# Activations rounded once where a norm makes them, token projections in rounded parts, and experts taken four at a time

## The reference

```python
# first_block, per layer
h = rmsnorm(x, norm1_g[l]);  p = h @ w_in[l]
y_rw, y_ret, y_sg = rwkv7_branch(p_rw, ...), retention_branch(p_ret, ...), sgu_branch(p_sg, ...)
x = x + jnp.sum(sigmoid(gate_logits) * proj(y_rw, y_ret, y_sg), axis=2) @ w_out[l]
x = x + conv_ffn(rmsnorm(x, norm2_g[l]), ffn_w_up[l], ...)
# second_block
u = rms_norm(x, mix_norm_g) @ w_in          # conformer convolution and dilated attention
x = x + mixed @ w_out
x = x + memory_cross_attention(rms_norm(x, xattn_norm_g), rms_norm(mem, mem_norm_g), w_q, w_k, w_v, w_o)
x = x + hierarchical_moe(rms_norm(x, moe_norm_g), ...)
```

## Time and profile before

| | before |
|---|---|
| median of 3 runs | 4093.9 us (4088.15 to 4098.93) |
| the profiled execution's own time | 4100.52 us |
| its span, first to last instruction | 4098.5 us |
| busy: TensorE, its weight loads | 81%, 58% |
| busy: DVE, ACT, POOL | 33%, 23%, 23% |
| mean granted TensorE clock, share of 2.4 GHz | 0.893 |
| read from HBM | 398.42 MB, mean 98 GB/s |

### The profile page before, as it was taken

The page is one execution under the profiler, slowest core; times in us unless marked ns, Lnnn a source line. Parts: engine busy times, 40 slices in busy tenths (PEclk is TensorE's granted clock), DMA queues, the critical chain, the costliest instruction groups (busy, mean ns, idle before and its releaser), DMA issues. The chain is left out here.

```text
span 4098.5 us, 51376 instructions
## 1 busy us (share of the span) xinstructions
PE 3321.2 (81%) x20124; PEld 2357.0 (58%) x20125; DVE 1336.1 (33%) x2111; ACT 936.4 (23%) x1279; POOL 949.0 (23%) x640
## 2 busy tenths in 40 slices
PE   6497668979998759665997999739786777999997
PEld 5296455657876638534665887427334655554553
DVE  2643332124420274333113441261752232122122
ACT  2322211124421232121112442211232121000001
POOL 2020002324442311100322444111201322212220
PEclk9698779999999879877998999869788887999999
DMA  2001111212231100111222223011002203888884
GB/s 96 11 4 53 47 64 62 87 67 83 95 113 50 59 5 24 41 47 54 92 72 67 98 93 112 21 43 63 0 0 72 103 31 136 344 353 339 330 330 168
DMA packets 53861, 402.60 MB, mean 98 GB/s; under 512 B 7249, under 2 KB 8273, under 8 KB 14417
## 3 DMA queue, kind: packets, MB, share of 16 engines
q1 hardware_dynamic: 53712, 400.54, 25.6%
HBM read 398.42 MB, written 2.10 MB: 98 GB/s over the span
## 5 line engine op out<-in xcount | busy, mean ns | idle before, releaser
L232 POOL TENSOR_TENSOR w_lo<-w,w_hi 128x1024 fp32r<-128x1024 f32 (+1 forms) x268 | 725.0, 2709 | 2024.1 <-ACT w_hi L227 2024.1
L250 PE MATMUL bank<-rhs_hi,w_hi 128*128 128x512 f32 (+1 forms) x2016 | 542.3, 414 | 227.1 <-DVE rhs_hi L238 191.1
L250 PEld LDWEIGHTS bank<-rhs_hi,w_hi 128*128 128x128 f32 x2016 | 393.1, 198 | 340.3 <-issue 215.5
L227 ACT CAST w_hi<-w 128x1024 fp32r<-128x1024 f32 (+1 forms) x268 | 302.8, 1137 | 1028.4 <-PE bank L259 910.8
L255 PE MATMUL bank<-rhs_lo,w_hi 128*128 128x512 f32 (+1 forms) x2016 | 509.1, 396 | 31.0 <-DVE rhs_lo L241 31.0
L259 PE MATMUL bank<-rhs_hi,w_lo 128*128 128x512 f32 (+1 forms) x2016 | 496.8, 389 | 0.0
L255 PEld LDWEIGHTS bank<-rhs_lo,w_hi 128*128 128x128 f32 x2016 | 383.6, 193 | 120.9 <-DVE rhs_lo L241 42.8
L259 PEld LDWEIGHTS bank<-rhs_hi,w_lo 128*128 128x128 f32 x2016 | 380.1, 191 | 78.3
L1988 PE MATMUL bank<-moe_w,moe_hg 128*64 128x512 f32 x1024 | 222.9, 592 | 0.8 <-issue 0.8
L2081 DVE TENSOR_TENSOR xT<-xT,bank 128x512 f32<-128x512 f32 x128 | 87.8, 686 | 238.5 <-PE bank L2033 238.2
L1988 PEld LDWEIGHTS bank<-moe_w,moe_hg 128*64 128x64 f32 x1024 | 88.3, 137 | 131.8 <-issue 131.8
(11 more groups left out here) (372 smaller groups left out, 4054.4 us busy)
## 6 DMA issues: line engine op xcount, KB each, us to landing
moe_w<-in_moe_w SPq DMA_DIRECT2D x128, 1024.0 KB, 12.6
moe_w<-in_moe_w SPq DMA_DIRECT2D x32, 2048.0 KB, 12.5
w<-in_w_in SPq DMA_DIRECT2D x45, 1024.0 KB, 4.9
w<-in_ffn_up SPq DMA_DIRECT2D x44, 1024.0 KB, 4.9
w<-in_w_merge SPq DMA_DIRECT2D x24, 1536.0 KB, 6.5
w<-in_ffn_down SPq DMA_DIRECT2D x16, 1408.0 KB, 5.9
w<-in_w_out SPq DMA_DIRECT2D x24, 512.0 KB, 3.5
w<-in_w_xk SPq DMA_DIRECT2D x4, 1024.0 KB, 6.0
```

The source lines that it names most:

```text
L227: self.nc.scalar.copy(self.w_hi[:, t, :, :], raw).then_inc(self.sems["w_hi"], 1)
L232: self.nc.gpsimd.tensor_tensor(self.w_lo[:, t, :, :], raw, self.w_hi[:, t, :, :].bitcast(F32), ALU.subtract).then_inc(self.sems["w_lo"], 1)
L250: self.nc.tensor.matmul(bank, hi[:, t, k, :], self.rhs_hi[:, k, :], start=(k == 0), stop=False)
```

## The change

Three things are changed together.

1. **Parts from the norm.** `norm_phase` gets `parts=(hi, lo)`: DVE scales into a scratch tile, ACT casts the high part, DVE subtracts, tile by tile. The parts stay resident (`h_hi` over `hT`'s place, `h_lo` in a tile of its own) and go to all the phases that read this norm's result; these no longer call `split.rhs`. The output projections (`down_phase` with `merged`, `mixed`, `ox`) still split their own operand. The memory's norm writes parts 256 wide.
2. **Projection by tokens in parts.** The chunk is cut along the contraction: half t holds four of the eight feature tiles with all 256 columns. ACT casts and POOL subtracts a half; TensorE runs three products over it for all token tiles.
3. **Experts in fours.** `h_tok` becomes `h_hi` and `h_lo` (the latter over `T.w`, free by then). One gather serves four experts (256 selection columns, two rounded products for each pair of tiles). `selg` goes: the turned 0/1 selection scatters, y is multiplied by the slot's gate when it leaves PSUM and split in two parts, and the gates by slot come from one-column matmuls (`sum_gates`). The weights are still fetched pair by pair, by the same waits. Scatter is spread over the next up.

`rwkv_prep_phase` also puts its small weights `up` into slot 0 of `T.w` instead of a tile of its own. In the diff, `merge_phase` and `ffn_up_phase` change as `project_phase` does, and `step(k)` calls `scatter(g, k - 1)` for k = 1 to 6.

```diff
@@ norm_phase @@
             rsqrt(act, sems["rooted"], 0, rstd[:, :], T.ps[0][:, 0:width], 1.0 / (tiles * P), T.eps(eps))
+            if parts is not None:
+                for k in range(tiles):
+                    act.wait_ge(sems["scaled"], k + 1)
+                    nc.scalar.copy(parts[0][:, k, 0:width], sq[:, k, :]).then_inc(sems["hi_ready"], 1)
...
             for k in range(tiles):
-                nc.vector.scalar_tensor_tensor(out=dst[:, k, :], in0=src[:, k, :], scalar=gain[:, k:k + 1],
-                                               in1=rstd[:, :], op0=ALU.mult, op1=ALU.mult)
+                out = dst[:, k, :] if parts is None else sq[:, k, :]
+                nc.vector.scalar_tensor_tensor(out=out, in0=src[:, k, :], scalar=gain[:, k:k + 1],
+                                               in1=rstd[:, :], op0=ALU.mult, op1=ALU.mult).then_inc(
+                                                   sems["scaled"], 1)
+                if parts is not None and k > 0:
+                    dve.wait_ge(sems["hi_ready"], k)
+                    nc.vector.tensor_tensor(parts[1][:, k - 1, 0:width], sq[:, k - 1, :],
+                                            parts[0][:, k - 1, 0:width].bitcast(F32), ALU.subtract)
...
@@ project_phase @@
-        split = Split(nc, ctx, T, sems, kt, width=width)
+        split = Split(nc, ctx, T, sems, kt, *parts, width=width)
...
-            pe.wait_ge(sems["rhs_hi"], kt)
...
-            split.rhs(dve, rhs)
...
@@ token_project_phase @@
-                sync.wait_ge(sems["dve_took"], 2 * i + s + 1)
+                sync.wait_ge(sems["w_lo"], 4 * i + 2 * s + 2)
...
-                pe.wait_ge(sems["w_full"][s], 16 * i + 16)
                 pe.wait_ge(sems["act_took"], 2 * i + s + 1)
                 pe.wait_ge(sems["dve_took"], 2 * i + s + 1)
-                for m in range(tiles):
-                    for k in range(KD):
-                        mm = nc.tensor.matmul(T.ps[4 * s + m][:, 0:256], lhs[:, k, m * P:m * P + P],
-                                              T.w[:, s, k * 256:k * 256 + 256], start=(k == 0), stop=(k == KD - 1))
+                for t in range(2):
+                    n = 4 * i + 2 * s + t
+                    pe.wait_ge(sems["w_hi"], n + 1)
+                    for lhs, w in ((split.rhs_hi, w_hi), (split.rhs_lo, w_hi), (split.rhs_hi, w_lo)):
+                        if w is w_lo:
+                            pe.wait_ge(sems["w_lo"], n + 5)
+                        for m in range(tiles):
+                            for k in range(half):
...
+                                mm = nc.tensor.matmul(T.ps[4 * s + m][:, 0:256],
+                                                      lhs[:, half * t + k, m * P:m * P + P], w[:, t, k, :],
+                                                      start=first, stop=last)
...
@@ route_phase @@
             for m in range(4):
-                act.wait_ge(sems["turned"], 2 * m + 1)
-                nc.scalar.copy(M.h_tok[:, m, 0:512], T.ps[2 * (m % 2)][:, :]).then_inc(sems["act_took"], 1)
+                for half in range(2):
+                    act.wait_ge(sems["turned"], 2 * m + half + 1)
+                    nc.scalar.copy(M.h_hi[:, m, 512 * half:512 * half + 512],
+                                   T.ps[2 * (m % 2) + half][:, :]).then_inc(sems["act_took"], 1)
...
-                v.tensor_copy(M.h_tok[:, m, 512:1024], T.ps[2 * (m % 2) + 1][:, :]).then_inc(sems["dve_took"], 1)
+                    v.tensor_tensor(M.h_lo[:, m, o], T.ps[2 * (m % 2) + half][:, :], M.h_hi[:, m, o].bitcast(F32),
+                                    ALU.subtract).then_inc(sems["dve_took"], 1)
...
@@ experts_phase, TensorE @@
+            def gather(q, s):
+                pe.wait_ge(sems["sel_ready"], q + 1)
+                for n in range(4):
+                    pe.wait_ge((sems["hg_act"], sems["hg_dve"])[n % 2], 2 * q + n // 2 + 1)
+                    for k in (2 * n, 2 * n + 1):
+                        for m in range(4):
+                            for part in (M.h_hi, M.h_lo):
+                                mm = nc.tensor.matmul(hg_banks[n % 2][:, (k % 2) * W4:(k % 2) * W4 + W4],
+                                                      part[:, m, k * P:k * P + P], sel[:, s, m, :],
                                                      start=(m == 0 and part is M.h_hi),
                                                      stop=(m == 3 and part is M.h_lo))
+                    mm.then_inc(sems["gathered"], 1)
...
+            def scatter(g, k):
+                pe.wait_ge(sems["added"], KD * g + k + 1)
+                nc.tensor.matmul(add_banks[k % 2][:, :], y_hi[:, k * P:k * P + P], selT[:, :], start=True, stop=False)
+                nc.tensor.matmul(add_banks[k % 2][:, :], y_lo[:, k * P:k * P + P], selT[:, :], start=False,
+                                 stop=True).then_inc(sems["scattered"], 1)
...
+            for q, s, more in quads_and_more(pe):
+                for b in range(2):
+                    g = 2 * q + b
+                    if b == 1 and more:
+                        gather(q + 1, 1 - s)
+                        sum_gates(q + 1, 1 - s)
+                    turn_and_down(g, s, b)
...
+                        up(g + 1, 1 - b, step)
...
+                    scatter(g, 6)
+                    scatter(g, 7)
```

More of the change, by code:

```diff
@@ L359, in _, with token_project_phase, raw @@
                 write(nc.vector, 2 * i + s, 1, T.ps[2 * s + 1][:, 0:width]).then_inc(sems["dve_took"], 1)
-def token_project_phase(nc, T, sems, stale, weights, chunks, lhs, write, tiles=4, ahead=None):
-    with nc.Block() as block:
+def token_project_phase(nc, T, sems, stale, weights, chunks, parts, write, tiles=4, ahead=None):
+    half = KD // 2
+    with ExitStack() as ctx:
+        split = Split(nc, ctx, T, sems, KD, *parts)
+        w_hi, w_lo = (w.rearrange("p t k c -> p t (k c)").rearrange("p t (k c) -> p t k c", k=half)
+                      for w in (split.w_hi, split.w_lo))
+        block = ctx.enter_context(nc.Block())
+        def raw(s, t):
+            return T.w[:, s, t * half * 256:(t + 1) * half * 256].rearrange("p (k c) -> p k c", k=half)
         @block.sync
@@ L394, in _, with high @@
             act.sem_inc(sems["act_took"], 2)
-            for i, s in two_slots(act, chunks):
+            def high(i, s, t, first=False):
+                act.wait_ge(sems["w_full"][s], 16 * i + 16)
+                if not first and t == 0:
+                    act.wait_ge(sems["half_done"], 2 * i + s)
+                if not first and t == 1:
+                    act.wait_ge(sems["odd_done"], (2 * i + s) * (tiles // 2))
+                nc.scalar.copy(w_hi[:, t, :, :], raw(s, t)).then_inc(sems["w_hi"], 1)
+            high(0, 0, 0, first=True)
+            high(0, 0, 1, first=True)
+            for (i, s), behind in with_next(act, chunks):
+                if behind:
+                    high(*behind, 0)
                 for m in range(0, tiles, 2):
@@ L1102, with ffn_up_phase @@
 FFN_UP_SEMS = SPLIT_SEMS + " loaded gate_done val_done gate_taken val_taken conv_done silu_done made dve"
-def ffn_up_phase(nc, T, sems, stale, weights, layer, hT, made_hi, made_lo, ahead):
+def ffn_up_phase(nc, T, sems, stale, weights, layer, parts, made_hi, made_lo, ahead):
     done = (sems["gate_done"], sems["val_done"])
@@ new lines, in _ @@
+            gated(0)
+            for q, s, more in quads_and_more(dve):
+                for b in range(2):
+                    g = 2 * q + b
+                    if b == 1 and more:
+                        rows(q + 1, 1)
+                        rows(q + 1, 3)
+                    for half in range(2):
+                        o = slice(512 * half, 512 * half + 512)
+                        dve.wait_ge(sems["y_hi"], 2 * g + half + 1)
+                        nc.vector.scalar_tensor_tensor(out=y_lo[:, o], in0=y_banks[half][:, :],
+                                                       scalar=slot_gate[:, s, b:b + 1], in1=y_hi[:, o].bitcast(F32),
+                                                       op0=ALU.mult, op1=ALU.subtract).then_inc(sems["y_lo"], 1)
+                    for k in range(6):
+                        add(g, k)
+                    if b == 0 or more:
@@ L2118, in block_two @@
         part = lambda name, first=0: (lambda c: pick(d[name], c + first))
-        norm_phase(nc, T, norm2, norm, xT, gain("mix_norm_g_2"), hT, ahead=fetch_first(T, pa, chunk, part("w_in_2")))
+        norm_phase(nc, T, norm2, norm, xT, gain("mix_norm_g_2"), None, ahead=fetch_first(T, pa, chunk, part("w_in_2")),
+                   parts=parts)
         with nc.sbuf_tensor([P, KD, S], F32) as mixed:
```

369 lines of the change are left out of this document (205 added, 164 removed).

## The result

The kernel with the change takes 3938.7 us (median of 4 runs, 3935.0 to 3942.6); the kernel before, run beside it, 4093.1 (4 runs). The ratio is 0.9622 with a 95% interval of 0.9605 to 0.9639: 154 us or 3.8% faster. The forecast was 3905, with a range of 3872 to 3955. The profiled execution took 3935.0 us, its span 3933.2.

The account below looks back on a forecast made before the run. TensorE's work and its idle stretches between phases were taken as the bound, TensorE itself in the experts. Starts and norms 82, token projections 21 and experts 86 make 189: 4100.5 to 3911.5, as a median 3905; range 3872 to 3955.

Parts of the forecast that it names:

- Starts without a norm ahead: At phase starts, DVE's casts and subtractions go: 9.5, 7.2 or 11.5 us gained each, 2 at one, 82.3 in sum.
- the clock mostly stays: At gate and cross-attention query starts, the shortened gap mostly keeps TensorE's clock: 9.5 us gained each, some 8 if it falls.
- Rival 2: At phase starts, the clock falls in shortened gaps and ScalarE or SP is late: 82 becomes 40, 3947 us; chance 0.12.
- Norms: Norms that write parts take 11.3 us on the DVE, 5.9 longer; with what follows, -0.7 us together.
- Ahead of the FFN it is a draw: At the norm before the FFN, TensorE begins 5.9 us later but no longer stops 5.13 for a low part.
- Token projections: 416 f32 products each become three rounded ones at 0.120 us: 31 gained, net 21, bounds -34 and 27.
- rival 3: In token projections and gathers, weight loads aren't hidden at 256 columns: 197 us lost, 4102; chance 0.02.
- a warm tile takes 5.44 us: At phase starts, a tile at full clock was priced at 5.44 us, read from the trace before the change.
- Experts: In the experts, a quad takes 62.6 us, 31.3 a pair for 37.23: 86 gained, bounds 62 and 98.
- six of eight go between the steps of the next up: In the experts, scatter's 16 rounded products at 0.227 us take 3.6 for 7.87, most of them placed within up.
- the walk: In the experts, a quad's steps added up: 62.6 us, with 2.85 between up and down for its first pair, 12.7 second.
- Rivals 1, 4 and 5: Experts bound by transfers, 3945 us, chance 0.13; clock falls in experts, 4150, 0.03; weights or selections too late, 4090, 0.02.

Follow-up runs that it names:

- experiment 4: The change's kernel padded so that rounded weights and both resident parts begin at the same place modulo 256 bytes: 3921.5 us, ratio 0.9573.
- experiment 1: The change's kernel with the kernel before's route and experts: 4005.9 us, ratio 0.9779; the kernel before with the experts in fours alone: 4032.3 us, ratio 0.9840.

## Why the prediction was right, and where it was not

Direction and range were right, the value 34 us too low. That the time lies inside the range is in part luck: the two terms missed below, 31 and 20 us, make 3956 of 3905, just outside it, and smaller misses the other way brought it back. The prediction's narrower range, 3882 to 3938, ended where the median came out, and its working doesn't give it: half of the distances to the bounds, 34 and 101 us, would have been 3888 to 3955.

- **Starts without a norm ahead.** Right in mechanism and nearly in size. By checkpoints of the two traces the two gate projections gained 9.3 each (9.5 forecast), the four retention and SGU starts 8.3, 8.3, 8.0 and 7.2 (7.2), the cross-attention query 8.3 (9.5). The merges began 12 us earlier but gave 2 to 3 back by their end. The assumption "the clock mostly stays" held only in part. Of the nine gaps of 2.1 to 2.4 us ahead of token projections, gates and query, four kept it (the query and three token projections), five were followed by a fall to the 1.2 GHz level: both gates (1.7 us each) and three token projections (about 1.5 each). Three gaps of 2.28 kept it and one of 2.28 didn't, so the length of the gap alone doesn't decide. Rival 2 happened in that part, at a small share of its price.
- **Norms.** The DVE stretch is 10.5 us for 11.3. The cross-attention norm lost 5.0 (5.9), mix gained 2.0 (1.2). "Ahead of the FFN it is a draw" came out at 3.0 and 3.2 lost. That isn't the norm's: 44 tiles at 5.547 for 5.440 are 4.7 of it.
- **Token projections.** 21.5 for 21, chunks of 11.4 for 11.5. At full pace products of 256 columns stayed 0.12 apart with their loads hidden: rival 3 didn't happen.
- **The pitch, a term that was missing.** I took "a warm tile takes 5.44 us" from the earlier trace rows as a property of the product. It was one of the placement, and the change moves the operands. It cost 20 us (agreement modulo 256 in experiment 4). The starts, norms and token projections would else have come out above their forecast; their total of 90 (93 in medians) for 103 is 20 lost and some 10 gained elsewhere. Those 10 can't be assigned to a term: two traces of the same code before the route differ by up to 11 us at its first product (3323.4 here, 3334.4 in the run of experiment 1). Of the pair of traces used here 4.7 us lie in the second block's attention, whose code no run changes and which took 207 to 215 us from trace to trace.
- **Experts.** This is the step that failed: "six of eight go between the steps of the next up", priced at the bare products. Their durations were right (0.227, and 0.121 in the gather, and the gates took 1.0 a quad, under the 2.2); the order was not free. Each of six changes a pair costs 0.35 us, 4.2 a quad, 31 in all, and the experts brought 62 to 67 for 86. With one change a pair within up a quad takes 62.66, so the rest of the walk held in sum: two changes are still in it (0.7) and the gates are 1.2 less. The earlier trace rows showed each kind of product only in runs of its own shape, 16 to 64 long; I had no row for a change and gave it no bound.
- **Transfers and clock in the experts.** Rivals 1, 4 and 5 didn't happen: share 0.92, clock 1.00.

The two missed terms add to 51, the miss is 34; what made up for it is the 10 us above and the gates (eight quads of 1.2).

## What to carry over

Where products of different shape are woven into each other on TensorE, count the changes of shape as well as the products, and put them in batches as large as the banks allow. When an operand is moved to another place, the time of the product may move with it: look at the spacing of single products in each phase, not at the mean of a group, and lay stationary and moving operand of long product streams at the same place modulo 256 bytes. A forecast that prices by rows should ask of each row in what neighbourhood and at what addresses it was taken.

## What the runs showed of the hardware that I had not expected

- A change between products on column halves (64 columns) and on the full array costs 0.35 us for the way there and back, with one or two products between; weight loads aren't hidden there. A change of format adds nothing to it: the excess was 2.53 - 2.17 = 0.36 with format and shape changing, and 2.92 - 1.72 - 0.85 = 0.35 with shape alone (0.85 is a full fp32 product, whose two records stand 0.43 apart in merge). Merge mixes both formats on the full array, and its tile of 8.893 in the kernel before is 24 x 0.2267 + 8 x 0.429 = 8.87 with next to nothing for the changes.
- Rounded products (fp32r) of 512 columns settle at 0.2267 us apart when the addresses of their two operands agree modulo 256 bytes, and up to 0.233 otherwise in the mean over a tile (5.600/24); a shift by 32 bytes cost the kernel before 34 us. The Trainium skill ("SBUF — State Buffer", Who interferes with whom) gives TensorE separate read ports for the moving operand and the weight load. The runs show that their addresses still bear on each other; whether through the ports isn't shown.
